# A hybrid encoder layer: long convolutions and mLSTM heads ordered step by step by the planner, prompt half by prompt half

## The reference, cut to what matters

```python
def encoder_layer(x, ...):
    h = rmsnorm(x, norm1_g)
    proj = h @ w_in
    cp = dwconv3(proj[..., :CONV_CH], conv_w, conv_b)
    x1, x2, hv = ...                       # 512 channels each, of cp
    kspec = hyena_filter_spectrum(S, ...)
    y_hy = hyena_mix(x1, x2, hv, kspec, hy_bias)
    q, k, v, o, gates = ...                # 4 heads of 128
    hm = mlstm_bidir(q, k, v, gates)
    hm = hm * lax.rsqrt(jnp.mean(jnp.square(hm), axis=-1, keepdims=True) + EPS)
    y_ml = o * hm.reshape(B, S, ML_WIDTH) * ml_norm_g
    x = x + jnp.concatenate([y_hy, y_ml], axis=-1) @ w_out
    u = dwconv3(rmsnorm(x, norm2_g) @ w_up, ffn_conv_w, ffn_conv_b)
    val, gate = u[..., :D_FF], u[..., D_FF:]
    return x + (jax.nn.silu(gate) * val) @ w_down

def hyena_mix(x1, x2, v, kspec, bias):     # two long convolutions, by their spectra
    z = x1 * long_conv(v, kspec[:, 0], bias[0])
    return x2 * long_conv(z, kspec[:, 1], bias[1])
```

## Time and profile before

| | us |
|---|---|
| median of 3 runs (2574.67 to 2578.0) | 2577.33 |
| the profiled execution | 2579.32 |
| its span | 2577.7 |
| PE busy / DVE busy / ACT busy over the span | 2315.3 / 1181.1 / 772.1 |
| second stage: first to last matmul | 780.3 to 1198.1 |

### The profile page before, as it was taken

How to read it: one execution, slowest core, us unless ns; L and a number is a source line. 1 busy time by engine, 2 the same in 40 slices (tenths; PEclk the granted TensorE clock), 3 DMA queues, 4 the chain that set the end, 5 groups by cost and what they waited for, 6 DMA issues and landing times. The chain is left out here.

```text
span 2577.7 us, 26949 instructions
## 1 busy us (share of the span) xinstructions
PE 2315.3 (90%) x10340; PEld 1878.6 (73%) x10340; DVE 1181.1 (46%) x1584; ACT 772.1 (30%) x1117; POOL 148.0 (6%) x164
## 2 busy tenths in 40 slices
PE   5999999998986898885886999999999993998997
PEld 3778788886864676664665788888888882787786
DVE  5675775446532776654235333333333333323332
ACT  4423322244433335433124222222221112212321
POOL 0211211000101100000000000000000000000000
PEclk9999999999998999997997999999999996999999
DMA  4344444434438667545241111111111113434442
GB/s 124 102 143 128 138 129 149 147 106 123 136 102 286 185 205 207 159 109 159 87 156 49 50 53 56 57 57 57 57 57 57 57 41 110 135 101 136 145 134 76
DMA packets 207474, 294.14 MB, mean 114 GB/s; under 512 B 13816, under 2 KB 142200, under 8 KB 207130
## 3 DMA queue, kind: packets, MB, share of 16 engines
q1 hardware_dynamic: 194842, 243.41, 32.2%
q0 software_dynamic: 11392, 46.41, 4.9%
q10 hardware_dynamic: 1152, 3.15, 0.3%
HBM read 201.09 MB, written 65.87 MB: 104 GB/s over the span
## 5 line engine op out<-in xcount | busy, mean ns | idle before, releaser
L128 PE MATMUL up_acc<-up_h_hi,up_w_hi 128*128 128x512 f32 x1056 | 412.1, 390 | 3.1 <-DVE up_w_lo L323 3.1
L129 PE MATMUL up_acc<-up_h_lo,up_w_hi 128*128 128x512 f32 x1056 | 411.8, 390 | 0.0
L130 PE MATMUL up_acc<-up_h_hi,up_w_lo 128*128 128x512 f32 x1056 | 411.7, 390 | 0.0
L245 DVE SCALAR_TENSOR_TENSOR up_u<-up_acc,up_conv_par,up_u 128x1023 f32<-128x1023 f32 x88 | 85.4, 1012 | 463.4 <-ACT up_u L311 463.4
L128 PE MATMUL down_acc<-down_w_hi,down_s_hi 128*128 128x512 f32 x528 | 209.3, 396 | 54.1 <-DVE down_w_lo L489 41.2
L128 PEld LDWEIGHTS up_acc<-up_h_hi,up_w_hi 128*128 128x128 f32 x1056 | 198.9, 188 | 44.7 <-issue 3.4
L130 PEld LDWEIGHTS up_acc<-up_h_hi,up_w_lo 128*128 128x128 f32 x1056 | 198.8, 188 | 41.4
L129 PEld LDWEIGHTS up_acc<-up_h_lo,up_w_hi 128*128 128x128 f32 x1056 | 199.0, 188 | 41.2
L311 ACT ACTIVATE up_u<-up_acc,up_conv_par 128x1536 f32<-128x1536 f32 x44 | 72.0, 1635 | 516.6 <-PE up_acc L130 516.6
L129 PE MATMUL down_acc<-down_w_lo,down_s_hi 128*128 128x512 f32 x528 | 208.0, 394 | 0.0
L130 PE MATMUL down_acc<-down_w_hi,down_s_lo 128*128 128x512 f32 x528 | 207.6, 393 | 0.0
(11 more groups left out here) (236 smaller groups left out, 3865.8 us busy)
## 6 DMA issues: line engine op xcount, KB each, us to landing
down_s_raw<-g_scratch SPq DMA_DIRECT2D x24, 1408.0 KB, 6.8
in_w_raw<-arg_w_in_t SPq DMA_DIRECT2D x58, 512.0 KB, 3.7
up_w_raw<-arg_w_up_t SPq DMA_DIRECT2D x44, 512.0 KB, 3.5
g_scratch<-up_prod POOLq DMA_DIRECT2D x22, 768.0 KB, 3.5
filt_tab<-arg_fwd SPq DMA_DIRECT2D x32, 512.0 KB, 3.8
mix_classes<-mix_split SPq DMA_DIRECT2D x48, 256.0 KB, 5.2
mix_kf<-k_scratch SPq DMA_DIRECT2D x48, 256.0 KB, 2.9
mix_split<-mix_classes SPq DMA_DIRECT2D x48, 256.0 KB, 4.8
```

The lines of the kernel that those rows point to most:

```text
L128: pe.matmul(out, w_hi, x_hi, start=first, stop=False)
L129: pe.matmul(out, w_hi, x_lo, start=False, stop=False)
L130: return pe.matmul(out, w_lo, x_hi, start=False, stop=last)
L245: dve.scalar_tensor_tensor(u[:, t0 + 1:t0 + n], acc[:, t0:t0 + n - 1], w_prev, u[:, t0 + 1:t0 + n], ALU.mult, ALU.add).then_inc(half_step, 1)
```

## The change

The hand-written list is gone. Each engine's instructions are now single steps of their own (`turn_k` and `score` where `keys` was, `attend` in each direction, `load_head`, `to_split` a block), grouped in some thirty streams of fixed inner order, and the planner `plan`, which already orders the first stage, merges the streams: again and again it takes the step that can start first by its table of durations and needs (`work`). With `even=True` equal starts go to the stream that is least far along. What every stream may do is fixed by `outer` and `inner` below; the order of turns is (0,0) (0,2) (1,0) (1,2) (0,1) (0,3) (1,1) (1,3): one prompt half through both orders with one sample half, then the others. The instructions of each kind, their shapes and the transfers stay the same in number. The first stage's order is the same as before. At the front of the stage the tables `tab` and the gates are now loaded ahead of the first head's data.

```diff
-    turns = [(0, 0), (0, 2), (0, 3), (1, 0), (1, 2), (1, 3), (0, 1), (1, 1)]
+    turns = [(0, 0), (0, 2), (1, 0), (1, 2), (0, 1), (0, 3), (1, 1), (1, 3)]
-    lag, ring = 2, 3
-    turn_at = {(0, 0): 12, (0, 2): 16, (0, 3): 20, (1, 0): 28, (1, 2): 32, (1, 3): 36}
+    ring = 3
...
+    outer = splits(0) + splits(2)
+    for turn in ((0, 0), (0, 2), (1, 0)):
+        outer += joined(*turn)
+    outer += splits(1) + joined(1, 2) + splits(3)
+    for turn in ((0, 1), (0, 3), (1, 1), (1, 3)):
+        outer += joined(*turn)
...
+    inner = keys_of(0)
     for j in range(len(jobs)):
...
+        inner += [("link", j, i) for i in range(nt - 1)] + [("attend", j, i, d) for i in range(nt) for d in range(DIRS)]
+        inner += (keys_of(j + 1) if j + 1 < len(jobs) else []) + [("turn_head", j, i) for i in range(nt // quad)]
...
+    def work(step):
...
+        if kind == "load_z":
+            return "SP", 0.6, 5.0, [("turn", 0, len(blocks(0)) - 1)] if a[0] == 1 else []
...
+        if kind == "load_tab":
+            return "SP", 0.6, 6.0, []
...
+        if kind == "multiply":
+            return "DVE", 2.1, 0, [("forward", a[0]), ("load_k", a[0])] + ([("inverse", a[0] - 2)] if a[0] >= 2 else [])
+        if kind == "inverse":
+            return "PE", 1.8, 0, [("multiply", a[0])] + ([("copy_classes", a[0] - 1)] if a[0] else [])
...
+        if kind == "to_split":
+            return "SP", 0.7, 5.5, [("copy_classes", last_pair[a[:2]])]
...
             @block.sync
             def _(sp):
...
+                load_z(0)
                 for s in range(len(SEQS)):
                     sp.dma_start(otab[s][:, :, :], outer_tab[s]).then_inc(sem["otab_loaded"], 16)
-                load_z(0)
+                load_z(2)
+                load_z(3)
...
-                load_head(0)
-                load_z(2)
-                load_z(3)
-                for step in schedule:
...
+                for step in order:
+                    if step[0] in loads and step not in started:
+                        loads[step[0]](*step[1:])
```

More of the change, by code:

```diff
@@ L1649, in outwards @@
         return [x for i in range(nt // 2) for x in (nt // 2 - 1 - i, nt // 2 + i)]
-    conv = []
-    def split_all(o, st):
-        conv.extend([("split", 0.9, o, st, b) for b in blocks(st)])
-    def pair_step(g, count):
-        if g - lag >= 0 and (g - lag) < len(pairs):
-            conv.append(("inverse", 1.8, g - lag))
-            for o, st in turns:
-                if last_pair[o, st] == g - lag:
-                    conv.append(("back", 0, o, st))
-        if g < count:
-            conv.append(("forward", 0.9, g))
@@ L1665, in join_all, with joined @@
-    def join_all(o, st):
+    def joined(o, st):
         nb = len(blocks(st))
+        out = []
         for b in range(nb + 2):
             if b < nb:
-                conv.append(("join", 0.9, o, st, b))
+                out.append(("join", o, st, b))
             if b >= 2:
-                conv.append(("split", 0.9, 1, st, b - 2) if o == 0 else ("turn", 0.3, st, b - 2))
-        if o == 1:
-            conv.append(("store", 0, st))
-    for st in (0, 2, 3):
-        split_all(0, st)
-    conv.append(("gap", 12))
@@ L1713, in spread, with splits @@
-    def spread(one, other):
-        out, at = [], 0
-        for i, x in enumerate(one):
-            out.append(x)
-            upto = len(other) * (i + 1) // len(one)
-            out += other[at:upto]
-            at = upto
-        return out
-    heads += keys_of(0)
+                out.append(("split", 1, st, b - 2) if o == 0 else ("turn", st, b - 2))
+        return out
+    def splits(st):
+        return [("split", 0, st, b) for b in blocks(st)]
+    outer = splits(0) + splits(2)
+    for turn in ((0, 0), (0, 2), (1, 0)):
+        outer += joined(*turn)
@@ L1729, in long_convolutions_and_heads @@
-        size = nt / 8
-        norm = [("magnitude", 0.5, j), ("shares", 0.3, j), ("weight", size, j, 0), ("weight", size, j, 1), ("add", size, j),
-                ("square", size, j), ("reduce", size, j), ("root", 0.5, j), ("unit", size, j)]
-        heads += spread(norm, keys_of(j + 1)) if j + 1 < len(jobs) else norm
-        heads += [("turn_head", 0.5, j, i) for i in range(nt // quad)] + [("store_head", 0, j)]
-    gaps = sum(x[1] for x in conv if x[0] == "gap")
-    share = (sum(x[1] for x in heads) - gaps) / sum(x[1] for x in conv if x[0] != "gap")
@@ L1787, in long_convolutions_and_heads @@
+    v_at, y_at, t_at = ({x[1:]: n for n, x in enumerate(y for y in outer if y[0] == kind)} for kind in ("split", "join", "turn"))
+    vy_of = {step: n % 2 for n, step in enumerate(outer)}
+    aged_at = {x: n for n, x in enumerate(aged)}
     with ExitStack() as ctx:
```

386 lines of the change are left out of this document (195 added, 191 removed).

## The result

The changed kernel is slower: 2601.3 us in the median of four runs (2599.4 to 2610.0) against 2577.7 us (2574.7 to 2579.3) for the kernel before on the same chip. The ratio is 1.010, with a 95% interval from 1.0074 to 1.0125. The forecast was 2563 in a range up to 2589, so both sign and range were missed. The profiled execution took 2599.4 us, 34 more than the 2565 that the sum gives for one.

The account below looks back on a forecast made before the run. PE has most work in the middle stage, 291 of 418 us, and the change can alter only the 126 us lost. Terms +3.5 - 9.4 + 21.5 - 30 = -14 us turn the median 2577.3 into 2563; range 2537 to 2589.

Parts of the forecast that it names:

- the landing of the class transfers: Front of the middle stage: class transfers land about 6.7 us after issue, putting the first forward at 824.5.
- forward 36's wait: Second half of the middle stage: PE waits 2 us at forward 36.
- The front: Middle stage's start to the first forward: 29.6 us lost, 3.5 more than before; first forward at 824.5, bounds 821 to 837.
- The first pairs: First forward to forward 8: 3.3 us lost in place of 12.7, 9.4 less; forward 8 at 856.5.
- The rest of the first half: Forward 8 to the split of stream 1: 36 us lost against 14.8, 21.5 more; that split at 988.
- the first join's wait: Join (0,0,0), after inverse 7: 6 us of waiting for transfers back, plus 2.5 at the lower clock.
- `z`: Load of `z` for stream 1, before its split: 7.5 us of waiting and 2 at the lower clock.
- forward 12: Turn (1,0): its last class transfer lands about 4 us after PE gets to forward 12.
- the joins of (1, 0): Joins of (1,0) in the first half: 2.5 us of waiting for the transfers.
- The second half: Split of stream 1 to the stage's end: 43 us lost against 72.7, 30 less; end at 1184.
- Transfers on SP's one queue, slower: Rival: bulk loads ahead make class transfers land 7 us later at four prompt turns, 28 us; 2591, chance 0.23.
- The dense stage: Rival: class and back transfers were long only from loads queued beside them; some 28 us of waits go; 2535, chance 0.17.

Follow-up runs that it names:

- run 2: Changed kernel with POOL's mask waiting on its own semaphore for the two e-row loads instead of all five head loads: 2587.5 us, ratio 1.0032.
- run 9: Changed kernel with head 5, gate (1, 1) and head 6's o-row loads moved on SP behind class transfers, mask wait unchanged: 2595.8 us, ratio 1.0078.
- run 6: Changed kernel with the mask's own semaphore, and loads of head 5, gate (1, 1) and head 6's o rows behind class transfers: 2572.1 us, ratio 0.9984.
- run 12: Changed kernel with the mask's own semaphore, all bulk loads behind prompt turns' class transfers, and trace-based planner prices for head load and mask: 2558.3 us, ratio 0.9931.
- run 10: run 6 with two gates and the o rows of heads 0 and 1 moved behind the class transfers of (0, 0): 2565.4 us, ratio 0.9954.
- runs 3 and 8: Changed kernel with the old order of turns: 2601.3 us, ratio 1.0088; the same plus the mask's own semaphore: 2595.0 us, ratio 1.0066.
- run 11: Changed kernel with the mask's own semaphore and every gate, o-row and later head load within prompt turns' class transfers moved behind them: 2570.6 us, ratio 0.9973.

## Why the prediction was wrong

Two steps failed. The first is a term put at nothing: PE's waits for copies that stand on ScalarE behind exponentials, a mask and a head's load; the runs showed three such waits of 5.9 to 7.1 us and 14 to 16 us for them. The second is a term that was mis-sized: the landing of the class transfers, taken at 6.7 us, and forward 36's wait, taken at 2; at three of the four prompt turns they landed later, up to 14.9 us after their issue, and putting the bulk loads behind them gave 15 us at two turns and 7 in the front.

The same account of lost time as above, for the runs with the changed kernel's turns. PE's work up to the marks is the same in all but the last, where the new prices move 6 us of it out of the front:

| lost, us | to the first forward | to the split of stream 1 | to the end | sum |
|---|---|---|---|---|
| forecast | 29.6 | 39.6 | 43 | 112 |
| changed kernel | 37.1 | 51.8 | 61.5 | 150 |
| run 2, ScalarE freed | 37.8 | 36.8 | 61.6 | 136 |
| run 9, three moves alone | 39.1 | 50.2 | 47.7 | 137 |
| run 6, both | 38.1 | 40.5 | 41.0 | 120 |
| run 12, all | 30.8 | 39.0 | 36.2 | 106 |

*The front, forecast +3.5, first forward at 824.5.* It came at 829.3, within the bounds of 821 to 837 but 7.5 us of loss above the term; 3 of these come of the stage's earlier first matmul, from which the loss is counted. The bytes ahead of the head's data were counted well: POOL's mask began at 802.9 (805 forecast, though from a first issue 3.5 us earlier), and the copy of split 7 was through at 814.3, before the 818 charged. The mis-sized step is the landing behind it. I charged 6.7 us for the last class transfer of (0, 0):

```profile
mix_classes<-mix_split SPq DMA_DIRECT2D x1, 256.0 KB, 14.9
```

It took 14.9 (transfers issued 813.4 to 815 us), with `o` rows, 1.5 MB of the second table and other class transfers issued just before it. Run 10 showed 7 us of it in the gates and `o` rows.

*The first pairs, forecast -9.4, forward 8 at 856.5.* Right in the main: from the first forward to forward 8 (829.32 to 863.16) passed 33.8 us for 28.7 of work, 5.1 lost where 3.3 were charged and 12.7 before.

*The rest of the first half, forecast +21.5, split of stream 1 at 988.* Of the terms that I named the first join's wait came as sized, 6.31 us (6 charged). The others were too high: `z` 4.58 (7.5 charged), forward 12 no wait (4 charged), the joins of (1, 0) 1.0 (2.5 charged). (The terms as listed add to 36.0, which makes 21.2 and not 21.5; nothing hangs on it.) The step that failed is the one that isn't there: ScalarE's two stalls at 894 and 989, 14 us of waiting on PE and 2 to 3 us at the low clock behind each. They cost more than the 12.2 us by which this part missed; the terms that were too high hid the rest. I had followed this chain in the front (mask, exponential, copy) and priced it there, but did not follow it through the list of ScalarE for heads 2, 4 and 6, where the same three kinds of step stand next to each other. With the mask's own semaphore this part loses 36.8 (run 2), against 39.6 forecast.

*The second half, forecast -30, end at 1184.* The form was right, and with both causes away the part loses 41.0 (run 6) where I charged 43. Some of that nearness is luck: 6 us were charged for the transfers at (0, 1), and the join waited 3.44 (1081.44) in the changed kernel. Here one of my terms was mis-sized: "forward 36 a wait of 2" was 7.84 us, and forward 24's 5.23 were not charged. The stall of 5.94 at 1099 is the first failed step again. In run 2 the stall at 1099 was gone and this part lost as much as before: PE came to forward 36 earlier by what it had gained in the first half, and still waited 7.6 us. Only the order on SP freed it (run 6).

*The rivals.* "Transfers on SP's one queue, slower" put the time at 2591 by bulk loads ahead of class transfers at each of four prompt turns. It is a good part of what happened. It asked for class transfers landing 7 us later than the 6.7 of the earlier trace rows; the last ones of the four prompt turns landed after 14.9, 4.7, 9.6 and 10.9 us, so at three turns 3 to 8 us later, and the two of the second half cost PE 5 and 8 us. Its chance of 0.23 was too low, since the prediction itself noted that nothing else is left to fill in. That the measured time came out beyond this rival's 2591 is the work of ScalarE's stalls, which no rival named. The sign given for it, forwards 12 and 36 waiting over 8 us, did not come: forward 12 had no wait, forward 36 waited 7.84 us.

The dense stage's reason, that transfers are slow only because other loads are queued beside them, is borne out for the class transfers (run 6) but not for those back: the first join waited 6.1 to 7.2 us in every run with these turns. There the measured 12.4 us were the right price: 12.3 us passed in the changed kernel (863.32 to 875.60). The estimate by the Trainium skill (DMA: Bandwidth & Descriptors, "Anatomy of one DMA — SWDGE (gpsimd) path"), 6.8 us from its 2 us and 436 GB/s, does not agree with this; it is for the GpSimd path, and the prediction had rightly not taken it. DMA's share in 800 to 990 us was named as a sign too, above 0.7; it was 0.62.

So the loss of the changed kernel is not in its order of turns (runs 3 and 8), but in the planner's prices for a head's load and mask, and in that it does not see what a bulk transfer does to those behind it on the queue. With these put right, the changed kernel beats the kernel before with the same mask semaphore: ratios of 0.9931 and 0.9969, some 10 us. Part of that may be the front, whose bulk loads were not moved in the kernel before; what its hand-written order would gain by that was not tried.

## What to carry to other kernels

When a planner makes the order, hold each of its prices against a trace, the longest chains first: here a load priced at 7.5 us took 14.8, and everything that an in-order engine had behind its consumer paid for it. For each step that can wait long (an exponential behind a mask behind a load), read what stands behind it on its own engine and who needs that, at every place where the same steps meet, not only at the first. Put loads that are needed late behind the transfers that an engine waits for; a planner that prices each transfer by itself doesn't see that. Do it where the trace shows such a wait: moving every one of them (run 11) was no better than moving seven (run 10).

## What the runs showed of the hardware

The DMA engines can be full at very different rates. Of the stretches below the first is from run 6, the second from the changed kernel while PE waits for forward 24:

```profile
1004.00:1008.00 4.00, 4.00 (x27) 3.64 (x27) 2.26 (x7) 3.15 (x9) 0.00 (x0) 1.00 1.07 207
...
1025.00:1029.00 4.00, 0.00 (x0) 0.00 (x0) 0.70 (x2) 1.96 (x8) 1.26 (x2) 1.00 0.97 266
```

The first stretch holds little but class transfers, the second also the head's load. With class transfers in the queues the engines are busy throughout (share about 1) at 207 to 266 GB/s, where the large table moved at 393. So bytes counted at the rate of the large table come out too short where transfers that cross partitions stand among them; in the changed kernel's front, too, the engines were full from 800 to 830 us (share 1.01) at 244 GB/s.

I had also not expected that a head's last load lands 11.9 us after its issue while its first, issued 3 us earlier, lands after 6.4: one semaphore for five loads makes the first wait for the slowest. Why the last takes that long is open.
